# Up-projections of the mixing layers as three passes on split operands, with their weights in the ring

## What is computed

```python
cq, ckv, kr = split(h @ w_in[:, last 416 columns], (256, 128, 32))
q  = rms_norm(cq,  g_q)  @ w_uq     # 256 -> 4 heads x (64 plain + 32 rotary)
kv = rms_norm(ckv, g_kv) @ w_ukv    # 128 -> 4 heads x (64 key + 64 value)
k  = [kv's key part, rope(kr)]      # the rotary part is the same in all heads
o  = softmax(q k^T * 96**-0.5) v
```

## Time and profile before

| | |
|---|---|
| device time, median of 3 runs (lowest to highest) | 1127.36 us (1127.21 to 1127.59) |
| profiled execution, its own time | 1127.63 us |
| its span in the profile | 1125.5 us |
| granted TensorE clock, mean | 0.999 of full speed |
| busy share of the span: PE, DVE, ACT, POOL | 99%, 69%, 48%, 10% |
| HBM read | 202 MB, mean 188 GB/s moved |

### The profile page before, as it was taken

One profiled execution on the slowest core, in us unless ns is written; L12 is line 12 of the kernel. 1 busy time (PEld: TensorE's weight loads), 2 busy tenths in 40 slices (PEclk: granted clock), 3 DMA queues, 4 the chain that ended last, 5 costly groups with the idle time before them and its releaser, 6 DMA issues.

```text
span 1125.5 us, 16761 instructions
## 1 busy us (share of the span) xinstructions
PE 1113.6 (99%) x6437; PEld 967.4 (86%) x6437; DVE 782.1 (69%) x1020; ACT 535.3 (48%) x705; POOL 108.7 (10%) x200
## 2 busy tenths in 40 slices
PE   8999999999999999999999999999999999999997
PEld 7888888898888888888998888888899988888886
DVE  6876666767667666678686676676776866766675
ACT  5533333556654333346685533333456755333332
POOL 2000000000000000002860000000038400000000
PEclk9999999999999999999999999999999999999999
DMA  8865556664356555568953465556699444665550
GB/s 257 266 223 188 184 189 209 221 206 138 123 169 226 187 185 188 188 185 245 252 155 118 163 225 187 187 185 197 179 244 223 108 151 148 212 201 186 186 186 37
DMA packets 174151, 211.22 MB, mean 188 GB/s; under 512 B 22387, under 2 KB 157107, under 8 KB 174098
## 3 DMA queue, kind: packets, MB, share of 16 engines
q1 hardware_dynamic: 164322, 202.89, 57.1%
q0 software_dynamic: 9776, 7.62, 3.6%
HBM read 201.98 MB, written 1.16 MB: 180 GB/s over the span
## 4 chain that ended last, share of the span: by engine, by line
PE 96%; DVE 1%; ACT 1%; issue 1%; DMA 1%; POOL 0%; SPq 0%; DVEq 0%; POOLq 0%; ACTq 0%
PE bank L1615 26%; PE bank L1619 14%; PE bank L1589 13%; PE bank L1590 13%; PE bank L1591 13%; PE bank L1693 4%; PE bank L1901 2%; PE bank L1922 2%; PE bank L1628 1%; PE bank L1759 1%; PE bank L1654 1%; PE bank L1932 1%; PE bank L1685 1%; PE bank L2141 1%; PE bank L1631 1%
## 5 line engine op out<-in xcount | busy, mean ns | idle before, releaser
L680 ACT ACTIVATE whi<-raw 128x2048 fp32r<-128x2048 f32 x178 | 338.9, 1907 | 384.9 <-PE bank L1619 245.5
L1002 DVE TENSOR_TENSOR wlo<-raw,whi 128x2048 fp32r<-128x2048 f32 (+1 forms) x173 | 394.8, 2285 | 149.3 <-ACT whi L680 149.2
L1615 PE MATMUL bank<-h_both,whi 128*128 128x512 f32 x1280 | 304.6, 390 | 0.0
L1615 PEld LDWEIGHTS bank<-h_both,whi 128*128 128x128 f32 x1280 | 237.7, 188 | 47.8
L1589 PE MATMUL bank<-whi,o_hi 128*128 128x512 f32 x448 | 176.2, 393 | 0.0
L1590 PE MATMUL bank<-wlo,o_hi 128*128 128x512 f32 x448 | 174.9, 390 | 0.0
L1591 PE MATMUL bank<-whi,o_lo 128*128 128x512 f32 x448 | 174.4, 389 | 0.0
L1619 PEld LDWEIGHTS bank<-h_both,wlo 128*128 128x128 f32 x1280 | 164.1, 191 | 6.2
L1619 PE MATMUL bank<-h_both,wlo 128*128 128x256 f32 x1280 | 166.0, 283 | 0.0
L1591 PEld LDWEIGHTS bank<-whi,o_lo 128*128 128x128 f32 x448 | 84.1, 188 | 18.0
L1589 PEld LDWEIGHTS bank<-whi,o_hi 128*128 128x128 f32 x448 | 84.3, 188 | 17.6 <-issue 1.3
(11 more groups left out here) (202 smaller groups left out, 1319.8 us busy)
## 6 DMA issues: line engine op xcount, KB each, us to landing
raw<-in_w_gate_up SPq DMA_DIRECT2D x44, 1024.0 KB, 5.1
raw<-in_w_down SPq DMA_DIRECT2D x44, 1024.0 KB, 4.9
raw<-in_w_gate SPq DMA_DIRECT2D x22, 1024.0 KB, 5.4
raw<-in_w_up SPq DMA_DIRECT2D x22, 1024.0 KB, 5.3
raw<-in_w_in SPq DMA_DIRECT2D x18, 1024.0 KB, 8.1
raw<-in_w_o SPq DMA_DIRECT2D x12, 1024.0 KB, 5.0
raw<-in_w_kv SPq DMA_DIRECT2D x8, 1024.0 KB, 5.5
raw<-in_w_q SPq DMA_DIRECT2D x4, 1024.0 KB, 5.0
```

The costliest lines, as they stand in the source:

```text
L680: act.activation(whi[:, s, 0:w], raw[:, s, 0:w], ACT.Copy).then_inc(hi_ready, 1)
L1002: dve.tensor_tensor(wlo[:, s, 0:w], raw[:, s, 0:w], whi[:, s, 0:w].bitcast(F32), ALU.subtract).then_inc(lo_ready, 1)
L1615: pe.matmul(bank[bk + jj][:, :], hi[:, kc, jj * P:(jj + 1) * P], h_both[:, kc, :, :].rearrange("p a t -> p (a t)"), start=(kc == 0), stop= ...
```

## The change

The up-projections are made like all other products: the transposed latents are kept as a high part (written by ACT) and a low part (three new DVE instructions of 128x256), both in `o_hi`, and the weights become a ring unit of their own, number 4 of the layer, 1536 wide, which moves all later units up by one (`ring`), so that the kernel has 181 units and not 179. TensorE's plain matmuls, 8 + 4 + 2 in a layer, become 24 + 6 + 6 matmuls on split operands: the keys of two heads at once into 128 rows of one bank. `load_layer` now stands ahead of the load of the unit after it, waits like a ring load, and issues eight DMAs, since the keys' and the values' columns go to separate places. In the script the split of unit 4 (and of 5) comes one TensorE unit later, and the split of the new unit stands before the copy of projection 2. The residual's four ACT instructions move from `latent_out` to behind `mla_G`; the bias loads that wait for them move behind the load of unit 7.

```diff
-FFN_U = [1, 50, 98, 146]
+FFN_U = [1, 50, 99, 148]
-MIX_U = [83, 131]
-N_UNITS = 179
+MIX_U = [83, 132]
+N_UNITS = 181
+UP_U = 4
+UP_W = 1536
@@ mix_script
-    s += unit(2) + [("near_low", 2), ("mla_T",)] + unit(3) + [("near_low", 3), ("mla_G",)] + unit(4)
+    s += [("unit", 2), ("up",), ("proj", 2), ("near_low", 2), ("mla_T",), ("unit", 3), ("split", 4), ("proj", 3)]
+    s += [("near_low", 3), ("split", 5), ("mla_G",), ("residual",)] + unit(4)
@@ tiles
-        wuq = sb("wuq", [P, 2, 4, P])
-        wukv = sb("wukv", [P, 4, 2, HD])
-        latT = xn[:, 1, 0:768].rearrange("p (c t) -> p c t", c=3)
+        latT_hi, latT_lo = o_hi[:, 0:3, :], o_hi[:, 3:6, :]
@@ helpers
+        def ring(l, n):
+            return MIX_U[l] + n + (1 if n >= UP_U else 0)
+        def up_weights(w, l):
+            s = slot_of(MIX_U[l] + UP_U)
+            return (w[:, s, 0:1024].rearrange("p (k h n) -> p k h n", k=2, h=4), w[:, s, 1024:1280], w[:, s, 1280:UP_W])
@@ SP, load_layer
-                if l:
-                    sp.wait_ge(mla_g, 3)
+                n = MIX_U[l] + UP_U
+                sp.wait_ge(lo_ready, n - 2)
+                wuq, wuk, wuv = up_weights(raw, l)
...
-                sp.dma_start(wukv[:, :, :, :].rearrange("p h a n -> p (h a n)"), a["w_ukv_2"][l]).then_inc(layer_in[l], 16)
+                ukv = a["w_ukv_2"][l].rearrange("p (h a n) -> p h a n", h=4, a=2)
+                sp.dma_start(wuk.rearrange("p (h n) -> p h n", h=4), ukv[:, :, 0, :]).then_inc(layer_in[l], 16)
+                sp.dma_start(wuv.rearrange("p (h n) -> p h n", h=4), ukv[:, :, 1, :]).then_inc(raw_in[slot_of(n)], 16)
@@ SP, loads of the layer
-                    load(mix_src(l, n), MIX_U[l] + n)
-                    if n == 0:
+                    if n == UP_U:
                         load_layer(l)
+                    load(mix_src(l, n), ring(l, n))
...
-                    if n == 5 and l == 0:
+                    if n == 7 and l == 0:
@@ ACT
+                    elif k == "up":
+                        act.wait_ge(layer_in[l], 16 * 7)
+                        split(u0 + UP_U)
@@ ACT, mla_T (the four instructions of the residual leave latent_out for a "residual" event)
-                            e = act.activation(latT[:, cc, :], bank[cc // 2][:, (cc % 2) * T:(cc % 2 + 1) * T], ACT.Copy,
+                            e = act.activation(latT_hi[:, cc, :], bank[cc // 2][:, (cc % 2) * T:(cc % 2 + 1) * T], ACT.Copy,
@@ ACT, mla_G
-                        for c2 in range(2):
-                            act.activation(qall[0:HD, 4 + 2 * c2:6 + 2 * c2, :], bank[2 + c2][0:HD, :].rearrange("p (c k) -> p c k", c=2), ACT.Copy)
-                        act.wait_ge(mla_g, 3 * l + 3)
+                        for r in range(2):
+                            act.activation(qall[0:HD, 4 + r:8:2, :], bank[2][HD * r:HD * r + HD, :].rearrange("p (c k) -> p c k", c=2), ACT.Copy)
+                        act.wait_ge(units_used, u0 + UP_U + 1)
@@ DVE
+                    elif k == "up":
+                        split(u0 + UP_U)
...
+                        dve.wait_ge(mla_tT, l + 1)
+                        for cc in range(3):
+                            e = dve.scalar_tensor_tensor(out=latT_lo[:, cc, :], in0=bank[cc // 2][:, (cc % 2) * T:(cc % 2 + 1) * T],
+                                                         scalar=mlag[:, l, cc:cc + 1], in1=latT_hi[:, cc, :].bitcast(F32),
+                                                         op0=ALU.mult, op1=ALU.subtract)
+                        e.then_inc(mla_tL, 1)
@@ TensorE, mla_G
-                        pe.wait_ge(mla_tT, l + 1)
-                        pe.wait_ge(layer_in[l], 16 * 7)
+                        pe.wait_ge(mla_tL, l + 1)
+                        pe.wait_ge(lo_ready, u0 + UP_U + 1)
...
-                                mm = pe.matmul(bank[h // 2][:, (h % 2) * T:(h % 2 + 1) * T], wuq[:, kc, h, :], latT[:, kc, :],
-                                               start=(kc == 0), stop=(kc == 1))
+                                mm = three(bank[h // 2][:, (h % 2) * T:(h % 2 + 1) * T], q_hi[:, kc, h, :], q_lo[:, kc, h, :],
+                                           latT_hi[:, kc, :], latT_lo[:, kc, :], kc == 0, kc == 1)
...
-                        for h in range(4):
-                            mm = pe.matmul(bank[2 + h // 2][0:HD, (h % 2) * T:(h % 2 + 1) * T], wukv[:, h, 0, :], latT[:, 2, :],
-                                           start=True, stop=True)
+                        for c2 in range(2):
+                            cols = slice(c2 * P, (c2 + 1) * P)
+                            mm = three(bank[2][:, c2 * T:(c2 + 1) * T], k_hi[:, cols], k_lo[:, cols],
+                                       latT_hi[:, 2, :], latT_lo[:, 2, :], True, True)
...
-                            mm = pe.matmul(bank[6][:, t * T:(t + 1) * T], latT[:, 2, tile(t)], wukv[:, :, 1, :], start=True, stop=True)
-                        mm.then_inc(mla_g, 1)
+                            mm = three(bank[6][:, t * T:(t + 1) * T], latT_hi[:, 2, tile(t)], latT_lo[:, 2, tile(t)], v_hi, v_lo, True, True)
+                        used(mm)
```

More of the change, by code:

```diff
@@ L313, in bass_two_stacks @@
         out_hi, out_lo = sem("out_hi"), sem("out_lo")
-        mla_sq, mla_ms, mla_rs, mla_lat, mla_t, mla_tT = (sem("mla_sq"), sem("mla_ms"), sem("mla_rs"),
-                                                          sem("mla_lat"), sem("mla_t"), sem("mla_tT"))
+        mla_sq, mla_ms, mla_rs, mla_lat, mla_t, mla_tT, mla_tL = (sem("mla_sq"), sem("mla_ms"), sem("mla_rs"),
+                                                          sem("mla_lat"), sem("mla_t"), sem("mla_tT"), sem("mla_tL"))
         latent_tile0 = sem("latent_tile0")
@@ L332, in bass_two_stacks @@
                     8: a["attn_norm_2"][1], 9: a["ffn_norm_2"][1], 10: a["final_norm_2"]}
-        LAST_U = {1: POOL_U, 2: FFN_U[0] + 32, 3: MOBA_U + 15, 4: FFN_U[1] + 32, 6: MIX_U[0] + 14,
-                  7: FFN_U[2] + 32, 8: MIX_U[1] + 14, 9: FFN_U[3] + 32}
+        LAST_U = {1: POOL_U, 2: FFN_U[0] + 32, 3: MOBA_U + 15, 4: FFN_U[1] + 32, 6: MIX_U[0] + 15,
+                  7: FFN_U[2] + 32, 8: MIX_U[1] + 15, 9: FFN_U[3] + 32}
         AFTER_FFN = (2, 4, 7, 9)
@@ L386, in width_of @@
         def width_of(n):
+            if n in (MIX_U[0] + UP_U, MIX_U[1] + UP_U):
+                return UP_W
             return LAT_K * LAT_W if n - MIX_U[0] in (0, 1) or n - MIX_U[1] in (0, 1) else UNIT
+        def ring(l, n):
[3 more added lines that the diff above has]
+            return (w[:, s, 0:1024].rearrange("p (k h n) -> p k h n", k=2, h=4), w[:, s, 1024:1280], w[:, s, 1280:UP_W])
         def slot_of(n):
@@ L902, in mix @@
                     if k == "split":
-                        split(u0 + ev[1])
+                        split(ring(l, ev[1]))
+                    elif k == "up":
+                        act.wait_ge(layer_in[l], 16 * 7)
+                        split(u0 + UP_U)
                     elif k == "proj":
@@ L922, in mix @@
                                 act.wait_ge(pv_done, hd0 + 4 * g)
-                            proj_copy(n, u0 + n, dst, bk[:, :], scale)
+                            proj_copy(n, ring(l, n), dst, bk[:, :], scale)
                     elif k == "latent_out":
@@ L935, in mix @@
                                                accum_out=msm[:, t, part:part + 1]).then_inc(mla_sq, 1)
+                    elif k == "mla_T":
+                        act.wait_ge(small_in, 15 * 16)
+                        act.wait_ge(mla_t, l + 1)
+                        for cc in range(3):
+                            e = act.activation(latT_hi[:, cc, :], bank[cc // 2][:, (cc % 2) * T:(cc % 2 + 1) * T], ACT.Copy,
+                                               scale=mlag[:, l, cc:cc + 1])
+                        e.then_inc(mla_tT, 1)
+                    elif k == "residual":
                         if l == 0:
@@ L941, in mix @@
                                     act.activation(x[:, t, cols], x_gained[:, t, cols], ACT.Copy, scale=rstd[:, t:t + 1]).then_inc(x_ready, 1)
[L942 to L945, removed]
-                            e = act.activation(latT[:, cc, :], bank[cc // 2][:, (cc % 2) * T:(cc % 2 + 1) * T], ACT.Copy,
-                                               scale=mlag[:, l, cc:cc + 1])
-                        e.then_inc(mla_tT, 1)
                     elif k == "mla_G":
-                        act.wait_ge(mla_g, 3 * l + 1)
+                        act.wait_ge(mla_g, 2 * l + 1)
                         for c2 in range(2):
@@ L954, in mix @@
                                            ACT.Copy, scale=MLA_D ** -0.5)
-                        act.wait_ge(mla_g, 3 * l + 2)
-                        for c2 in range(2):
-                            act.activation(qall[0:HD, 4 + 2 * c2:6 + 2 * c2, :], bank[2 + c2][0:HD, :].rearrange("p (c k) -> p c k", c=2), ACT.Copy)
-                        act.wait_ge(mla_g, 3 * l + 3)
+                        act.wait_ge(mla_g, 2 * l + 2)
```

(13 more changed lines are left out.)

2 lines of the change are left out of this document (added).

## The result

The kernel after takes 1134.57 us (median of 4 runs, 1132.68 to 1135.27) against 1127.31 (4 runs, 1127.21 to 1127.59) beside it: ratio 1.0060, interval 1.0048 to 1.0073. It is slower by 7.3 us. The forecast was 1124.2, the range 1122.5 to 1127.4; slower had a chance of 0.11. The profiled execution took 1134.54 us with a span of 1132.5, 7.0 us more than before.

A forecast was written before the change was run, and what follows sets the result against it. TensorE, busy 1113.6 of 1125.5 us, was taken as the bound. Matmuls 3.6 plus residual 0.9 less waits of 0.5 and 0.9 gave 3.1 us off the 1127.36 median: 1124.2 us, range 1122.5 to 1127.4.

The forecast's parts named there:

- Matmuls: At mla_G on TensorE, 36 split matmuls take 4.4 us instead of 6.2, saving 1.8 us per layer, 3.6 in all.
- Residual: Moving its four ACT instructions removes TensorE's wait for unit 3's low part in layer 0, a gain of 0.9 us.
- The new unit up to mla_G: Its loads, ACT split and DVE low parts finish before TensorE reaches mla_G, with 0.1 to 0.2 us of margin.
- Rival D: Slower: wuq's small loads land at 8.1 us, TensorE waits at mla_G; 1129.7 us, chance 0.12.
- Behind mla_G: Units 4 and 5 load later, so the first scores wait 0.5 us in layer 0 and 0.9 in layer 1.
- rival A: All cover holds, with no new waits: gain 4.5 us, 1122.9 us, chance 0.25.
- the terms 3.6 and 0.9: Gains in us: 3.6 from cheaper mla_G matmuls over both layers, 0.9 from moving the residual in layer 0.
- the waits of 1.4: First scores waiting for DVE's rotary work: 0.5 us in layer 0 and 0.9 in layer 1, subtracted from the gain.
- C: DVE's queue ahead of the first scores is the new bound: waits 1.2 and 2.2 us, 1125.6 to 1127.4, chance 0.27.
- The port: GpSimd's mask and unit 5's low part contend for SBUF: up to 0.75 us added per layer, gain 1.6 us.

The follow-up runs named there:

- e3: Kernel before, with only the residual's four ACT instructions and the two bias loads moved: 1126.26 us, ratio 0.9985.
- e1: Kernel after, with GpSimd's mask done on 4 of every 256 columns only, so its result differs: 1122.74 us, ratio 0.9961.
- e6: Kernel after, with GpSimd's mask moved behind load_near(3), the second half of its spreading DMAs: 1123.65 us, ratio 0.9961.
- e9: Kernel after, with GpSimd's mask done twice, 16 instructions for 8: 1136.97 us, ratio 1.0079.
- e7: e2 with each of GpSimd's eight mask instructions put between two of load_near(2)'s DMAs: 1123.87 us, ratio 0.9972.
- e2: Kernel after, with the split of unit 5 put behind mla_G in the script: 1124.84 us, ratio 0.9966.
- e10: Kernel after, with the mask in two rows of four and load_near(3)'s four DMAs between them: 1129.48 us, ratio 1.0015.
- e11: Kernel after, with the mask behind load_near(3) and the split of unit 5 behind mla_G, e6 and e2 together: 1128.74 us, ratio 1.0003.
- e4: Kernel after, with 14 unused matmuls of 512 columns on TensorE ahead of the first scores' wait in each layer: 1130.13 us, ratio 1.0019.
- e5: Kernel before, with GpSimd's mask applied a second time right after the first, sixteen instructions: 1127.92 us, ratio 1.0002.
- e12: Kernel before, with the mask ahead of load_near(2) instead of behind it: 1127.57 us, ratio 0.9999.
- e8: Kernel after, with each mask instruction put between two of load_near(2)'s DMAs, order of the splits unchanged: 1124.46 us, ratio 0.9973.

## Why the prediction was wrong

**Matmuls, right.** 1.9 us saved per layer (4.32 for 6.2), forecast 1.8. 36 records at mla_G, none of them late.

**Residual, right.** e3: 1.4 us for 0.9, with an interval that holds 0.9; its ACT instructions in the new place (537.58, 2.55 us in layer 0) made nobody wait.

**The new unit up to mla_G, held, with more margin.** wuq's loads landed in 2.4 to 2.9 us, not 4.7, and their six issues took 3.95 us of SP, not 6.5. In layer 0 ACT could begin on the unit at 524.62, forecast 525.5; the three low parts of the latents took 1.27 us, forecast 1.2, and ended at 531.06, forecast 531.8. TensorE came at 531.83 and waited for nothing, in both layers. Rival D is out.

**Behind mla_G, the step that failed.** The forecast had waits of 0.5 and 0.9 us there; they were 3.65 and 3.27. They had been worked out from landings of 8 us for units 4 and 5, the 0.9 of layer 1 as a middle between 1.3 to 2.2 and nothing. In layer 0 these units took 8.2 and 7.1 us to land, in layer 1 6.3 and 5.3. The low part of unit 5 was done at 537.11 in layer 0 of e1, forecast 538.2. With the mask cut down (e1) the rotary work ended at 541.41 and TensorE came at 541.89: no wait at all, and the time was 1122.74, rival A's 1122.9. So the terms 3.6 and 0.9 were right, and without the mask the waits of 1.4 would have been nothing. A stall of the first scores over 2 us was one of the signs of being wrong that the prediction gave, under C; its chance of slower stood on D, which did not happen.

**The port, mis-sized fivefold.** I had the mechanism, and the place: low part of unit 5 under the mask. I priced it at 0.75 us per layer at most, one mask instruction, and put it at nothing in the sum. It was 4.1 and 4.2 us, what was left of the whole row. I called the 0.86 us of the earlier trace rows agreement with the rule, and it was not. GpSimd of the kernel before, the two mask instructions in question:
```profile
537.43 0.76 POOL L613 TENSOR_TENSOR bias<-bias,nmask 128x256 f32<-128x256 f32 x1
...
538.11 0.76 POOL L613 TENSOR_TENSOR bias<-bias,nmask 128x256 f32<-128x256 f32 x1
```
The addition came at 537.89, during the first of them, and should have had the port at its end, 538.2. Its own 0.68 us, taken from its end at 539.43, began at 538.75: it was passed over once and got in behind the second. Once it can be passed over, one mask instruction is no bound. The next one in the rows is the row of eight at 6.0 us, and what is left of it should have been the upper end: 4 us more in each layer, against a margin of 0.5 in layer 0 (541.41 and 541.89 in e1). The Trainium skill (SBUF — State Buffer, section Who interferes with whom) says that whoever issues first has the shared pair "for the whole instruction". In e6 and in the second half of e9 the trace agrees (additions of 1.02 to 1.08 us, 0.4 over 0.68), and with e7's mask instruction of 2.39. In after, e2, e10 and e11 it does not: DVE was passed over at up to six boundaries between GpSimd's instructions, and in e7 (531.51) and e11 (536.20) it lost although the profile has it start first. The measurement decides, and the rule gives no upper bound for a row.

**The clock, left out.** I costed a stall at its own length. The stalls of 3.65 and 3.27 us of TensorE also cost 1.7 and 3.2 us through the 1.2 GHz level behind them (e4: 4.4 together). In the kernel before TensorE's longest wait was 1.5 us and the clock line shows no fall, and the prediction did not ask what a longer one would do.

**What stays open** is what decides whether DVE is let in. Length of the delayed instruction (e2), length of the row (e5, e9) and whether the row runs already (e12) are excluded as the single cause. What holds in every trace here: after GpSimd itself has once waited for DVE within a row, the two alternate to its end. And in a row where it had not yet, DVE got in behind the same instruction in both layers of a kernel: the 6th in the kernel before, e3 and e5, the 7th in e11, the 8th in after, e2, e4 and e9, the 4th of e10's fours. In e12 it was the 3rd in layer 0; in layer 1 DVE was there first. That looks like a place in GpSimd's instruction stream, but it was only observed, in one profiled execution of each kernel, and no run moved that place by itself.

## What to carry to other kernels

Before an instruction of DVE with two inputs in SBUF is moved, look what GpSimd runs at that time, and price the meeting by all that is left of GpSimd's row of back-to-back instructions, not by one of them; a meeting that cost 0.86 us before is no measure of the next. What worked here was to have the long instruction of DVE at the port well before the row (e6, by 1.1 us in layer 0), or to break the row with other work (e8). Where TensorE is the bound, add the clock to a stall: here one of 3.27 us cost twice its length, since the clock fell with it.

## What the hardware showed beyond that

TensorE's idle time did not by itself fix the clock. The fall came after 4.26 and 3.98 (e9), 3.65, 3.27, 2.83 (e10, layer 0) and 1.78 us (e11, layer 1), and not after 2.08 (e11, layer 0), 1.86 (e10, layer 1), 1.48 (e8) or 1.16 (e6). It fits that e11's runs spread: four took 1125.5 to 1125.9 us with a mean granted clock of 0.998 to 1.000, eight took 1128.3 to 1130.5 with 0.995 to 0.997. The runs of e6, at 0.998 to 0.999, lay within 0.7 us.

Two changes at one meeting place don't add: e2 gains 2.8 us on the kernel before, e6 3.9, both together nothing in the median. The fastest version that computes the whole result is e6, at 1123.65 us 3.9 us under the kernel before and 10.9 under the one after; e7, at 1123.87, cannot be told from it.
